# Sending the prompt products of neighbouring pairs of weight chunks side by side in an expert-choice mixture

## What is computed

```python
def expert_choice_ffn(x, w_router, w1, w3, w2):
    n = b * t
    cap = EC_FACTOR * n // N_EXPERTS                 # 128 sample tokens, 32 prompt tokens for each expert
    aff = jax.nn.softmax((xf @ w_router).astype(jnp.float32), axis=-1)
    top_aff, top_idx = lax.top_k(aff.T, cap)
    xe = xf[top_idx]
    hid = jax.nn.silu(jnp.einsum('ecd,edf->ecf', xe, w1)) * jnp.einsum('ecd,edf->ecf', xe, w3)
    ye = jnp.einsum('ecf,efd->ecd', hid, w2) * top_aff[..., None].astype(xf.dtype)
    out = jnp.zeros_like(xf).at[top_idx.reshape(-1)].add(ye.reshape(-1, d))
```

## Time and profile before

| | |
|---|---|
| median of 3 runs | 3601.62 us (3590.61 to 3605.51) |
| the profiled execution | 3599.11 us |
| its span, first to last instruction | 3597.3 us |
| mean granted TensorE clock, as a share of 2.4 GHz | 0.962 |
| PE busy | 3356.8 us (93%) |
| DVE busy | 2229.8 us (62%) |
| ACT busy | 1641.0 us (46%) |
| HBM traffic | 219 GB/s over the span |

### The profile page before, as it was taken

One profiled execution on the slowest core, in us unless ns is written; L12 is line 12 of the kernel. 1 busy time (PEld: TensorE's weight loads), 2 busy tenths in 40 slices (PEclk: granted clock), 3 DMA queues, 4 the chain that ended last, 5 costly groups with the idle time before them and its releaser, 6 DMA issues.

```text
span 3597.3 us, 54507 instructions
## 1 busy us (share of the span) xinstructions
PE 3356.8 (93%) x22416; PEld 2402.2 (67%) x22416; DVE 2229.8 (62%) x2849; ACT 1641.0 (46%) x2194; POOL 409.9 (11%) x326
## 2 busy tenths in 40 slices
PE   4878899989899967999999999999999999999997
PEld 2546788778777755666666666666666666666664
DVE  6764333177666466666666666666666666666666
ACT  2222322156312224555555555555555555555564
POOL 1330100011342220000000000000000000000000
PEclk8878999989999988999999999999999999999998
DMA  3455342253675345777777777777777777777786
GB/s 137 174 181 185 108 129 89 76 156 117 248 243 203 106 151 196 272 255 271 258 261 267 261 258 268 263 259 268 259 261 270 257 263 270 255 265 267 251 304 216
DMA packets 226035, 791.15 MB, mean 220 GB/s; under 512 B 28525, under 2 KB 35321, under 8 KB 221564
## 3 DMA queue, kind: packets, MB, share of 16 engines
q1 hardware_dynamic: 206028, 722.02, 57.6%
q0 software_dynamic: 19760, 65.65, 6.7%
HBM read 730.31 MB, written 57.26 MB: 219 GB/s over the span
## 4 chain that ended last, share of the span: by engine, by line
PE 61%; DVE 1%; DMA 0%; ACT 0%; POOL 0%; issue 0%; SPq 0%; ACTq 0%; POOLq 0%; DVEq 0%
PE exp_bank L2843 17%; PE exp_bank L2852 15%; PE exp_bank L2844 14%; PE exp_bank L2845 13%; PE exp_bank L2825 1%; PE exp_bank L2827 1%; PE exp_bank L2811 0%; DVE g_pick L2424 0%; DVE g_pick L2423 0%; DVE g_pick L2426 0%; DMA out_y<-exp_xb 0%; DMA exp_xq<-hidden_rows,g_rows_q 0%; DMA exp_xb<-residual 0%; PE exp_bank L2815 0%; POOL exp_xg L2586 0%
## 5 line engine op out<-in xcount | busy, mean ns | idle before, releaser
L126 DVE TENSOR_TENSOR exp_lo<-exp_raw,exp_hi 128x1024 fp32r<-128x1024 f32 x1056 | 1262.6, 1222 | 678.1 <-ACT exp_hi L122 672.2
L122 ACT ACTIVATE exp_hi<-exp_raw 128x1024 fp32r<-128x1024 f32 x1056 | 1061.7, 1052 | 958.7 <-PE exp_bank L2852 950.3
L2843 PE MATMUL exp_bank<-exp_hi,exp_xt 128*128 128x512 f32 (+1 forms) x1536 | 616.5, 401 | 1.0 <-DVE exp_xt L2693 1.0
L2844 PE MATMUL exp_bank<-exp_lo,exp_xt 128*128 128x512 f32 (+1 forms) x1536 | 580.2, 378 | 0.0
L2845 PE MATMUL exp_bank<-exp_hi,exp_xt 128*128 128x512 f32 (+1 forms) x1536 | 572.7, 373 | 0.0
L2843 PEld LDWEIGHTS exp_bank<-exp_hi,exp_xt 128*128 128x128 f32 x1536 | 288.9, 188 | 166.0 <-issue 114.3
L2852 PE MATMUL exp_bank<-exp_raw,exp_xtp 128*32 128x256 f32 (+1 forms) x6144 | 377.4, 367 | 0.0
L2845 PEld LDWEIGHTS exp_bank<-exp_hi,exp_xt 128*128 128x128 f32 x1536 | 290.2, 189 | 58.1
L2844 PEld LDWEIGHTS exp_bank<-exp_lo,exp_xt 128*128 128x128 f32 x1536 | 290.1, 189 | 40.5
L2843 PE MATMUL exp_bank<-exp_hi,exp_hid 128*128 128x512 f32 x704 | 296.9, 422 | 5.5 <-DVE exp_lo L126 5.5
L2844 PE MATMUL exp_bank<-exp_lo,exp_hid 128*128 128x512 f32 x704 | 279.0, 396 | 0.0
(11 more groups left out here) (419 smaller groups left out, 4558.3 us busy)
## 6 DMA issues: line engine op xcount, KB each, us to landing
exp_raw<-in_w SPq DMA_DIRECT2D x1056, 512.0 KB, 4.5
hy_table<-in_basis_s POOLq DMA_DIRECT2D x64, 512.0 KB, 5.0
carry_tiles<-in_w_ada SPq DMA_DIRECT2D x24, 1024.0 KB, 5.5
proj_raw<-in_w_in SPq DMA_DIRECT2D x24, 512.0 KB, 4.6
filt_raw<-in_kbasis_s SPq DMA_DIRECT2D x18, 512.0 KB, 6.0
spectrum_s<-filt_spec SPq DMA_DIRECT2D x34, 256.0 KB, 2.2
carry_flex<-spectrum_s SPq DMA_DIRECT2D x16, 512.0 KB, 4.0
features<-proj_xr SPq DMA_DIRECT2D x12, 512.0 KB, 3.0
```

Source lines behind the costliest of these rows:

```text
L122: act.activation(self.hi[:, c % self.ns, :], self.raw[:, c % self.nr, :], ACT.Copy).then_inc(self.hi_done, 1)
L126: dve.tensor_tensor(self.lo[:, c % self.ns, :], self.raw[:, c % self.nr, :], self.hi[:, c % self.ns, :].bitcast(F32), ALU.subtract).then_i ...
L2843: pe.matmul(out, xh, wh, start=(k == 0), stop=False)
L2844: pe.matmul(out, xh, wl, start=False, stop=False)
```

## The change

Pairs now alternate by the parity of c // 2. A pair with even c // 2 is sent as before: both samples, then both prompts. A pair with odd c // 2 is sent mirrored: both prompts, then both samples, and there the last sample product of each chunk releases the buffers. Before the mirrored pair's prompts PE waits for the raw chunk to have landed. `X_TURN` moves from 53 to 55, so that all transposes stand behind a mirrored pair. The prompt rows are now transposed over all 128 partitions, the lower 64 of which DVE sets to zero once at the start of the phase; ACT reads the halves it needs with another stride.

```diff
@@
-    X_TURN = 53
+    X_TURN = 55
@@ def hid_prompt(b):
-                    turn_p[:, 0:nf * CAP_P].rearrange("p (i l t) -> p i l t", i=nf // 2, l=2))
+                    turn_p[:, 0:nf * 64].rearrange("p (i l t) -> p i l t", i=nf // 2, l=NQ)[:, :, 2:NQ, :])
@@ def _(dve):
+            dve.memset(hdp[0:64, :], 0.0)
             choice.on_vector(dve, s_ix)
@@ def hid_transposes(e, b):
                 for i in range(nf // 2):
-                    tr = pe.transpose(turn_p[:, i * 64:(i + 1) * 64], hdp[64:128, i * 128:(i + 1) * 128], g["ident"][64:128, 64:128])
+                    tr = pe.transpose(turn_p[:, i * 128:(i + 1) * 128], hdp[:, i * 128:(i + 1) * 128], g["ident"][:])
@@ def prompts(e, i, c):
-                mm.then_inc(st.used, 1)
+                return mm
@@ the loop over pairs on PE
                     for c in range(c0, c1, 2):
-                        for x in (c, c + 1):
-                            st.ready(pe, e * NC, x)
-                            if i == NB and (x - c0) % 4 == 0:
-                                pe.wait_ge(s_hid, e * NB + (x - c0) // 4 + 1)
-                                pe.wait_ge(s_hp, e * NB + (x - c0) // 4 + 1)
-                            samples(e, i, x)
-                        for x in (c, c + 1):
-                            prompts(e, i, x)
+                        pair, f = (c, c + 1), c - c0
+                        if c // 2 % 2 == 0:
+                            for x in pair:
+                                st.ready(pe, e * NC, x)
+                                if i == NB and f % 4 == 0 and x == c:
+                                    pe.wait_ge(s_hid, e * NB + f // 4 + 1)
+                                    pe.wait_ge(s_hp, e * NB + f // 4 + 1)
+                                samples(e, i, x)
+                            for x in pair:
+                                prompts(e, i, x).then_inc(st.used, 1)
+                        else:
+                            for x in pair:
+                                pe.wait_ge(st.landed[x % st.nr], (e * (NC // st.nr) + x // st.nr) * 16 + 16)
+                                if i == NB and f % 4 == 0 and x == c:
+                                    pe.wait_ge(s_hp, e * NB + f // 4 + 1)
+                                prompts(e, i, x)
+                            for x in pair:
+                                st.ready(pe, e * NC, x)
+                                if i == NB and f % 4 == 0 and x == c:
+                                    pe.wait_ge(s_hid, e * NB + f // 4 + 1)
+                                samples(e, i, x).then_inc(st.used, 1)
```

More of the change, by code:

```diff
@@ L2844, in samples @@
                         pe.matmul(out, xh, wl, start=False, stop=False)
-                        pe.matmul(out, xl, wh, start=False, stop=(k == nk - 1))
+                        mm = pe.matmul(out, xl, wh, start=False, stop=(k == nk - 1))
+                return mm
             def prompts(e, i, c):
```

## The result

| | before | after |
|---|---|---|
| median | 3600.9 us (4 runs, 3590.6 to 3605.5) | 3470.8 us (4 runs, 3469.3 to 3476.8) |
| profiled execution | 3599.1 us | 3469.3 us |
| span | 3597.3 us | 3467.5 us |
| one expert, steady stretch | 137.36 us | 129.67 us |

The ratio is 0.9646, with a 95% interval of 0.9622 to 0.9669: **3.5% faster**. Not all of the 130 us is the change's: in the two profiles, 122.4 us lie behind the first transpose of gathered tokens, where the experts begin (2229.9 us before, 2107.5 after), and the rest ahead of it. The kernel before, run again beside the experiments, had medians of 3590.6 to 3594.8 us.

What follows compares the result with a forecast made beforehand. PE's own instruction row was taken as the bound. Savings 84.5 + 15.5, less 1, 0.3 and 1, gave 97.7 us: profiled 3599.1 to 3501.4, median 2.5 higher at 3504 us; range 3487 to 3545.

Steps and rivals of the forecast that it cites:

- A: Joints of two pairs on PE: the prompts' side loss of 0.15 us stays, time 3543 us; chance 0.10.
- B: Joints of two pairs on PE: nothing gained, weight loads stay open, only cheaper transposes count, 3588 us; chance 0.05.
- price of a round trip: PE's changes between samples and prompts: 0.33 us lost per pair, 0.18 on the samples and 0.15 on the prompts.
- C: Ends of experts: weights land late and PE stops, two stops per expert costing 219 us, 3723 us; chance 0.03.
- D: Ends of experts: small PE stops of a microsecond or two each, 30 us together, 3534 us; chance 0.06.
- the tail's: Last expert: PE's wait behind SP's store and load chain grows, so 1 us of the gain is lost.
- Step 1: PE's row in the experts: 256 round trips between samples and prompts go at 0.33 us each, 84.5 us less.
- Step 2: Turns of hidden rows: six whole-array transposes take 0.70 instead of 0.85 us, three 0.35 instead of 0.57; 15.5 us less.
- two other steps: Bounds for the transposes' entry behind samples (nothing or 8 us) and DVE's one-time zeroing (0 to 0.5 us).

Runs made afterwards that it cites:

- mirrored groups of four: Changed kernel's pairs replaced by groups of four chunks, every second group mirrored, with a separate semaphore for prompts; 3435.9 us, ratio 0.9539 to the kernel before.

## Why the prediction was wrong

**What held.** PE's own row is the limit, before and after. The joints cost nothing: rivals A (0.15 stays with the prompts) and B (nothing comes) are refuted by the group step of 0.22 at 1868.67; the rule of the Trainium skill quoted for B ("TensorE: Matmul & The Clock Gate", "The mechanism") does not hold here, since weight loads stay hidden at a joint of products that all use all rows: the step at the joint is the one within a pair. The loss goes with the change of form. The price of a round trip held too: 0.33 us against a step of 0.233. Nobody behind PE fell late (rivals C and D): the only new stop is the tail's, 0.67 us longer where 1 was forecast. 16 round trips per expert went.

**Step 1 was sized too small**: 84.5 us were forecast, and with the 18.7 us worked out here it was about 103. Its price was taken against a step of 0.233 within the samples, read from the twelve of one pair, and this was taken as what a longer run would have. It was a run that had not settled; a run of 24 samples behind 32 prompt records settles at 0.227. Of the 1.5 us per expert by which the forecast was short, 1.17 are this. With every step within the samples kept at 0.2325, two things shorten the samples. There are 16 fewer last samples in front of prompts (0.318 each), which gives 1.37 us. The first samples give 1.18: 26 of 0.341 and seven of up to 0.338 before, against 17 of 0.337 behind prompts and seven of about 0.313 behind transposes after. Together that is 2.55 us less, and 3.72 were measured. The difference is 18.7 us over 16 experts. The rows for it were in the trace: in the pairs behind a turn of hidden rows the last steps were 0.227 (the kernel before took 2.94 there at four of six turns, and 2.96 at two), and I looked at one pair only.

**Step 2 was sized too small**, by 0.31 us per expert or 5 us. The price of a transpose, 0.116, was worked out from a stretch that began with a change of form (its first step was 0.17), so it carried a part of the very loss that the change removes; measured, the step is 0.109. The same stretch was read as one in which the sample behind transposes loses nothing. Its first step was 0.316, and the last transpose in front of it took 0.03, so only the sum of the two shows no loss.

**The rest**, about 9 us, is for the most part the stretch ahead of the experts, 7.4 us, which the prediction took as fixed, and 1 us by which the median lay nearer to the profiled run than before; that part of the miss is luck of the runs and says nothing about the change. The experts' gain alone would have put the time at 3599.1 - 122.4 + 2.5 = 3479 us, still below the range. The range allowed 15 us for runs, but downwards only together with the bounds of two other steps, and its lower end had no case for a gain beyond the count. With the first two terms right the forecast would have been 3480 us.

## What to carry to other kernels

Count how often PE changes between whole-array products, strips and transposes that read part of the partitions, and send equal forms side by side: a round trip costs 0.33 us of PE's row here, which shortens a kernel only where PE is its limit, and padding a transpose to 128 partitions was cheaper than its narrow form (25 us over 96 turns). A step read from a short run is not the step of a long one: compare runs of different length, and what stands ahead of them, before a price is taken per instruction. What may stand side by side is set by when buffers come free, so a separate count for each kind of product lets groups grow, as the mirrored groups of four show.

## What the runs showed of the hardware

- A run of samples after strips begins with steps of 0.34 and 0.24 and settles at 0.227 us, after eleven samples behind 16 prompt records and after five behind 32, be they wide (1.86 us) or narrow (1.01 us). So the number of prompt instructions ahead counts, and not their time; behind transposes it took three to ten samples. Why, stays open.
- The loss in front of and behind strips is the same for runs of 16, 32 and 64 records: the last sample's step is 0.318, the last group's 0.329 (0.227 and 0.216 within a run).
- Transposes in full precision stand among samples of rounded operands without loss, as long as both use the whole array: the sample in front takes 0.232, and the last transpose and the first sample behind it 0.34 together, as 0.109 and 0.23 would.
- The part ahead of the experts, the same code in every kernel here, varied by 18 us between twelve profiles, and with it the time at the lower of the two clock levels, from 211 to 252 us.
